# Gated expert rows go into the residual stream by accumulating stores, and the projection starts from raw rows

## What is computed

```python
def trunk(x):
    for layer in (0, 1):
        xn = rms_norm(x, mix_norm_g[layer])            # x * rsqrt(mean(x*x) + eps) * g
        x = x + (even_mixer if layer == 0 else odd_mixer)(xn)
        x = x + hierarchical_moe(rms_norm(x, ffn_norm_g[layer]))
    return x

def hierarchical_moe(xn):                              # 1024 tokens
    grp_p, grp = top_1(softmax(xn @ wg_group + b))     # 4 groups
    top_p, local = top_2(softmax(e_logits[grp]))       # 8 experts in a group
    gate = grp_p * top_p / sum(top_p)                  # two gates a token
    expert = grp * 8 + local                           # 32 experts, 2048 slots
    y[slot] = (silu(x[tok] @ w_gate[e]) * (x[tok] @ w_up[e])) @ w_down[e]
    return sum over the token's two slots of gate * y[slot]
```

## Time and profile before

| | us |
|---|---|
| median of 3 runs | 2018.22 |
| the profiled execution | 2011.2 |
| its span, first to last instruction | 2009.6 |
| PE busy in the span | 1814.2 |
| DVE busy | 1194.1 |
| ACT busy | 883.8 |
| POOL busy | 321.3 |
| mean granted clock of TensorE | 0.948 of full speed |
| DMA, mean over the span | 186 GB/s |

### The profile page before, as it was taken

One profiled execution on the slowest core, in us unless ns is written; L12 is line 12 of the kernel. 1 busy time (PEld: TensorE's weight loads), 2 busy tenths in 40 slices (PEclk: granted clock), 3 DMA queues, 4 the chain that ended last, 5 costly groups with the idle time before them and its releaser, 6 DMA issues. The chain is left out here.

```text
span 2009.6 us, 26040 instructions
## 1 busy us (share of the span) xinstructions
PE 1814.2 (90%) x9786; PEld 1498.5 (75%) x9787; DVE 1194.1 (59%) x1603; ACT 883.8 (44%) x1062; POOL 321.3 (16%) x260
## 2 busy tenths in 40 slices
PE   8999999577999999889999956999999979999990
PEld 6888889476778878768887745888878857888770
DVE  4323434566665445669999857323235558999984
ACT  4102222263333332348888844111112137888870
POOL 0000000001000001134334300000000133344320
PEclk8999999778999999989999987999999989999995
DMA  5433332702000043479999957111306369999976
GB/s 204 142 121 121 113 131 70 170 1 85 1 1 1 1 158 135 171 291 362 376 373 378 355 217 249 42 52 42 94 13 216 105 253 349 381 385 374 371 283 260
DMA packets 144946, 374.18 MB, mean 186 GB/s; under 512 B 39886, under 2 KB 74830, under 8 KB 120094
## 3 DMA queue, kind: packets, MB, share of 16 engines
q1 hardware_dynamic: 113254, 309.38, 42.3%
q0 software_dynamic: 22368, 45.47, 6.3%
q10 hardware_dynamic: 9216, 17.93, 2.4%
HBM read 331.15 MB, written 75.10 MB: 202 GB/s over the span
## 5 line engine op out<-in xcount | busy, mean ns | idle before, releaser
L1345 PE MATMUL ex_ps_h<-even_split 128*128 128x512 f32 x768 | 194.5, 404 | 7.8 <-DVE even_split L1474 7.4
L1345 PE MATMUL ex_ps_h<-odd_split 128*128 128x512 f32 x768 | 193.1, 401 | 9.0 <-DVE odd_split L1474 7.2
L1345 PEld LDWEIGHTS ex_ps_h<-even_split 128*128 128x128 f32 x768 | 141.0, 190 | 46.8 <-DVE even_split L1474 13.6
L1345 PEld LDWEIGHTS ex_ps_h<-odd_split 128*128 128x128 f32 x768 | 140.4, 189 | 47.5 <-DVE odd_split L1474 13.9
L520 PE MATMUL in_ps<-in_w_hi,in_xT_hi 128*128 128x512 f32 (+1 forms) x448 | 172.2, 384 | 1.7 <-DVE in_xT_lo L425 1.7
L520 PE MATMUL in_ps<-in_w_lo,in_xT_hi 128*128 128x512 f32 (+1 forms) x448 | 169.0, 377 | 0.0
L520 PE MATMUL in_ps<-in_w_hi,in_xT_lo 128*128 128x512 f32 (+1 forms) x448 | 169.0, 377 | 0.0
L1749 PE MATMUL conv_ps<-conv_xT_hi,conv_w_hi 128*128 128x512 f32 x384 | 150.4, 392 | 0.9 <-DVE conv_w_lo L1687 0.9
L1749 PE MATMUL conv_ps<-conv_xT_lo,conv_w_hi 128*128 128x512 f32 x384 | 149.7, 390 | 0.0
L1749 PE MATMUL conv_ps<-conv_xT_hi,conv_w_lo 128*128 128x512 f32 x384 | 149.7, 390 | 0.0
L2470 ACT ACTIVATE att_prob<-att_ps_s 128x512 f32<-128x512 f32 x114 | 68.0, 598 | 151.4 <-PE att_ps_s L2405 151.2
(11 more groups left out here) (360 smaller groups left out, 4023.7 us busy)
## 6 DMA issues: line engine op xcount, KB each, us to landing
all_region<-in_moe_w_gate SPq DMA_DIRECT2D x16, 1024.0 KB
all_region<-in_moe_w_up SPq DMA_DIRECT2D x16, 1024.0 KB
all_region<-in_moe_w_down SPq DMA_DIRECT2D x16, 1024.0 KB
experts_w_gu<-in_moe_w_gate SPq DMA_DIRECT2D x16, 1024.0 KB
experts_w_gu<-in_moe_w_up SPq DMA_DIRECT2D x16, 1024.0 KB
experts_w_d<-in_moe_w_down SPq DMA_DIRECT2D x16, 1024.0 KB, 15.4
all_region<-in_ev_w_in SPq DMA_DIRECT2D x12, 1024.0 KB, 8.3
proj<-in_stage ACTq DMA_DIRECT2D x48, 256.0 KB, 2.1
```

Source lines behind the costliest of these rows:

```text
L1345: last = pe.matmul(ps_h[:, u % 2, :], a[:, u % 2, k, :], w[:, k, :], start=(k == 0 and j == 0), stop=(k == KT - 1 and j == 2))
```

## The change

What it does, part by part:

1. **Stores that accumulate.** The experts' results are no longer written to `slots`. ACT multiplies the rows by their gates on the way out of PSUM (a scale for each partition), and POOL's indirect DMA adds them into the residual stream in DRAM (`compute_op=ALU.add`), into `stream` for layer 0 and into `out` for layer 1. The destination index is the token. Experts are taken in the order 0, 8, 16, 24, 1, 9, ... (`EXPERT_AT`), so that four stores in a row go to four groups; before each store POOL waits for the store of four experts earlier.
2. **Gates by expert.** After the softmax the router multiplies the one-hot choices by the gates (DVE), PE makes 16 more products of 128x32 that list the gates by place and expert, and DVE copies the list. PE's last warm-up goes from 8 products to 2 and 2, ahead of and behind these. `coded` (two DVE operations for each tile) replaces the code factor in `placed_at`.
3. **No mixing.** `mix` and `finish` are gone, and so are the loads of `slots` and the store of `stream1`. The convolution stage's rows are loaded by SP's queue at the end of the experts' block, after all 32 stores have landed (`MixedRows.load`); its gains and first weights are loaded there too, before that wait.
4. **Raw rows in the input stage.** PE turns the raw rows; the gain goes into the weights (ACT's high part takes it as a scale, DVE's low part as a factor, in pieces of 512 columns), and 1/rms is applied when DVE takes the product. The first product is done in two halves of four pieces. The constants are made inside this block, at the head of POOL's stream.
5. **Retention steps** come in every tile of blocks 3 to 5, none in block 6. With its places free, SP's queue loads keys, gains, `peT`, `w1s`, `w2s` and `q_rows` during block 6, before the preparation block, and preparation starts its turning and `add_places` one step earlier.

The core of the diff:

```diff
 # input stage
-                    act.activation(w_hi[:, b % 2, at, 0:n], raw[:, c, :, 0:n], ACT.Copy).then_inc(hi_ready[c], 1)
+                    for k in range(HALF):
+                        act.activation(w_hi[:, b % 2, c * HALF + k, 0:n], raw[:, c, k, 0:n], ACT.Copy,
+                                       scale=gains_T[:, c * HALF + k:c * HALF + k + 1]).then_inc(hi_ready[c], 1)
-                    dve.scalar_tensor_tensor(xn[:, t % 2, :], xin[:, t % XS, :], rstd[:, t:t + 1], gains[:],
-                                             ALU.mult, ALU.mult).then_inc(normed, 1)
-                    dve.tensor_copy(stage[:, q % 4, 0:n], ps[:, q % BANKS, 0:n]).then_inc(staged, 1)
+                    dve.tensor_scalar(stage[:, q % 4, 0:n], ps[:, q % BANKS, 0:n], rstd[:, t:t + 1], None, ALU.mult
+                                      ).then_inc(staged, 1)
-            return divmod((b - GATE) * NT + t, 4) if b >= GATE else (None, None)
+            return divmod((b - GATE) * NT + t, 3) if GATE <= b < GATE + 3 else (None, None)
+                sp.wait_ge(y_done, NT)
+                sp.wait_ge(y_ready, NT)
+                for t in range(NT - 4, NT):
+                    in_memory(sp, KEYS, t)
+                ahead.load_first_keys(sp)
+                early.load_small(sp)
+                sp.wait_ge(multiplied, (KEYS + 1) * NT)
+                early.load_weights(sp)
+                for t in range(NT):
+                    in_memory(sp, KEYS + 1, t)
+                    ahead.load_second_keys(sp, t)
 # router
+                dve.tensor_tensor(chosen[:].rearrange("p c t e -> p (c t) e"), chosen[:].rearrange("p c t e -> p (c t) e"),
+                                  gates[:].unsqueeze(2).to_broadcast([P, 2 * NT, NE]), ALU.mult).then_inc(gates_placed, 1)
-                warm_up(pe, ps_o[:, 0, 0:COLS], cst.ident[:], hT[:, (NT - 2) % 2, 0:COLS // P, :].rearrange("p k n -> p (k n)"), 8)
+                warm_up(pe, ps_o[:, 0, 0:COLS], cst.ident[:], hT[:, 0:COLS // P, :].rearrange("p k n -> p (k n)"), 2)
+                pe.wait_ge(gates_placed, 1)
+                pe.wait_ge(logits_out, NT)
+                for t in range(NT):
+                    for c in range(2):
+                        last = pe.matmul(ps_g, placed_at[:, c, t, :], chosen[:, c, t, :], start=(t == 0 and c == 0), stop=(t == NT - 1 and c == 1))
+                last.then_inc(gates_listed, 1)
+                warm_up(pe, ps_o[:, 0, 0:COLS], cst.ident[:], hT[:, 0:COLS // P, :].rearrange("p k n -> p (k n)"), 2)
 # experts
+EXPERT_AT = [s % NG * EPG + s // NG for s in range(NE)]
+                def add_rows(w, at):
+                    if at >= NG:
+                        pool.wait_ge(scattered[(at - NG) % U], w * (16 * STEPS) + (16 * ((at - NG) // U) + 16))
+                    pool.wait_ge(y_out, w * NE + (at + 1))
                     pool.sem_inc(apart, 1)
                     pool.indirect_dma_start(
-                        out=slots, out_offset=bass.IndirectOffsetOnAxis(ap=idx[:, e, 1:2], axis=0),
-                        in_=y[:, e % 2, :], in_offset=None,
-                        bounds_check=last_slot, oob_is_err=False).then_inc(scattered[e % U], 16)
+                        out=stream, out_offset=bass.IndirectOffsetOnAxis(ap=idx[:, EXPERT_AT[at], 0:1], axis=0),
+                        in_=y[:, at % 2, :], in_offset=None,
+                        bounds_check=last_token, oob_is_err=False, compute_op=ALU.add).then_inc(scattered[at % U], 16)
-                    act.activation(y[:, u % 2, :], ps_y[:], ACT.Copy).then_inc(y_out, 1)
+                    act.activation(y[:, u % 2, :], ps_y[:], ACT.Copy, scale=lists.gate[:, ds(place_of(n, u), 1)]).then_inc(y_out, 1)
-                for piece in (SECOND, DOWN):
-                    sp.wait_ge(piece_lo[piece], NE - B + 1)
-                following.load(sp, range(NT - 2))
+                if following is not None:
+                    for piece in (SECOND, DOWN):
+                        sp.wait_ge(piece_lo[piece], NE - 1)
+                    following.load_weights(sp)
+                    for u in range(U):
+                        sp.wait_ge(scattered[u], 16 * STEPS)
+                    following.load(sp)
 # convolution stage
-                    act.wait_ge(mixed, t + 1)
+                    act.wait_ge(x_loaded[t], 16)
-                    for c in range(2):
-                        last = dve.scalar_tensor_tensor(xin[:, t, :], ya[:, t % YA, c, :], gates[:, t + c * NT:t + c * NT + 1],
-                                                        xin[:, t, :], ALU.mult, ALU.add)
 # the whole
-            finish(nc, "end", following[1], slots, gates, out)
```

More of the change, by code:

```diff
@@ L507, in turn, with first_product @@
                     for k in range(KT):
-                        last = pe.transpose(ps_t[t % 2][:, k, :], xn[:, t % 2, k * P:(k + 1) * P], cst.ident[:])
+                        last = pe.transpose(ps_t[t % 2][:, k, :], xin[:, t % XS, k * P:(k + 1) * P], cst.ident[:])
                     last.then_inc(turned, 1)
+                def first_product(c):
+                    pe.wait_ge(x_high, 1)
+                    for j, (a, w_part) in enumerate(((xT_hi, w_hi), (xT_lo, w_hi), (xT_hi, w_lo))):
+                        if j == 1:
+                            pe.wait_ge(x_low, 1)
+                        for k in range(c * HALF, (c + 1) * HALF):
+                            if j != 1:
+                                pe.wait_ge((hi_ready if j == 0 else lo_ready)[c], k - c * HALF + 1)
+                            last = pe.matmul(ps[:, 0, 0:COLS], a[:, k, 0:P], w_part[:, 0, k, 0:COLS],
+                                             start=(k == 0 and j == 0), stop=(k == KT - 1 and j == 2))
+                    if c == 1:
+                        last.then_inc(multiplied, 1)
                 def product(b, t):
@@ L592 @@
 EXPERT_BUFFERS = 4
+EXPERT_AT = [s % NG * EPG + s // NG for s in range(NE)]
+PLACE_OF = [EXPERT_AT.index(e) for e in range(NE)]
 class ExpertData:
@@ L1139, in load, with landed @@
             sp.dma_start(self.rows[:, t, :], self.src[t * P:(t + 1) * P, :]).then_inc(self.loaded[t], 16)
-    def load_again(self, sp, loaded):
+    def landed(self, sp):
         for t in range(NT):
-            sp.dma_start(self.rows[:, t, :], self.src[t * P:(t + 1) * P, :]).then_inc(loaded, 16)
-def experts(nc, name, data, lists, slots, most, ident, following):
+            sp.wait_ge(self.loaded[t], 16)
+        for sem in (*self.raw_loaded, self.gain_loaded):
+            sp.wait_ge(sem, 16)
@@ L1159, in experts, with load_again @@
+    def load_again(self, sp, again):
+        self.load_first(sp, [again] * 3, again)
+        for t in range(NT):
+            sp.dma_start(self.rows[:, t, :], self.src[t * P:(t + 1) * P, :]).then_inc(again, 16)
+        sp.wait_ge(again, 16 * (NT + 4))
+def experts(nc, name, data, lists, stream, most, ident, following=None):
     U, B = 8, EXPERT_BUFFERS
@@ L1322, in landed @@
                 def landed():
-                    for t in range(NT - 2, NT):
-                        pool.wait_ge(following.loaded[t], 16)
-                later_waves(pool, full, wave, landed)
+                    if following is not None:
+                        following.landed(pool)
+                    lists.store_gates(pool)
+                later_waves(pool, full, wave, landed, lambda: pool.sem_inc(all_scattered, 1))
             @block.tensor
@@ L1536, in mix_and_conv, with constants @@
[L1536 to L1541 removed]
+def constants(pool, cst, ident_ready):
+    pool.memset(cst.ident[:], 0.0)
+    pool.memset(cst.ones[:], 1.0)
+    pool.drain()
+    pool.affine_select(out=cst.ident[:], in_=cst.ident[:], compare_op=ALU.not_equal, fill=1.0, base=0,
+                       pattern=[[-1, P]], channel_multiplier=1).then_inc(ident_ready, 1)
+    pool.affine_select(out=cst.before[:], in_=cst.ones[:], compare_op=ALU.is_gt, fill=0.0, base=0,
+                       pattern=[[1, P]], channel_multiplier=-1)
+    pool.iota(cst.iota_i[:, 0, :], pattern=[[1, 64]], base=0, channel_multiplier=0)
+    pool.iota(cst.iota_i[:, 1, :], pattern=[[1, 64]], base=-64, channel_multiplier=0)
+    pool.drain()
+    pool.tensor_copy(cst.iota[:], cst.iota_i[:, 0, :])
+    pool.tensor_copy(cst.from_64[:], cst.iota_i[:, 1, :])
+    pool.drain()
@@ L1647, in _ @@
                 act.wait_ge(eps_ready, 1)
+                act.activation(root[:, 0:1], eps[:], ACT.Sqrt)
+                high(0, 0)
                 squares(0)
@@ L1812, in prepare_attention @@
+def prepare_attention(nc, name, proj, cst, con, keep, ahead, early):
     NK = 2 * G
@@ L2640, in trunk @@
             region = Region(top)
-            with nc.Block() as block:
-                constants(nc, cst, block)
             def expert_data(layer, m, region):
@@ L2646, in expert_data @@
                                   a["moe_w_down"][layer, :, :, :], region)
-            following = [NextRows(top, f"rows{layer}_loaded", stream[2 * layer], region) for layer in range(2)]
```

(2 more changed lines are left out.)

540 lines of the change are left out of this document (266 added, 274 removed).

## The result

The changed kernel takes 2034.3 us (median of 4 runs, 2033.51 to 2035.38) against 2017.3 us of the kernel before in the same session (4 runs). The ratio is 1.0075, 95% interval 1.0052 to 1.0098: **slower, by 17 us** by the medians, where 1996 was forecast and the range ended at 2028. Its profiled execution spans 2031.8 us; the one of before spanned 2009.6.

The account below looks back on a forecast made before the run. An expert stage was taken to sit on both limits, PE and DMA, at once. Edges of -54.8 us and accumulating stores of +32.4 us gave -22.4 us, from 2018.2 to 1995.8 us; the range was 1962 to 2028 us.

Parts of the forecast that it names:

- Accumulating stores: Expert stages: each adding store costs 0.6 us of DMA time over 27 rounds while weights are outstanding, +32.4 us for two layers.
- Rival 2: Expert stages: the store is dear, DMA engines lose over 1.0 us a store; at 1.4 us 2039 us; chance 0.17.
- the edges: Places outside the expert rounds where PE stands still, from input stage to finish: together -54.8 us.
- Rival 3: Expert stages: store landing passes 17 us and ACT's wait for `y` sets the round; 2039 us at 20 us; chance 0.03.
- Rival 1: Expert stages: the destination fetch is hidden, price 0 to 0.3 us a store; 1963.4 to 1980 us; chance 0.24.
- Rival 4: Convolution's start stays put and weights hold the input stage, so -54.8 becomes -43; 2008 us; chance 0.11.
- Rounds near 10.5, waits from about round 9: Expert stages, expected sign: ACT's waits for weights begin earlier, about round 9, with rounds near 10.5 us from there on.
- Input stage: Start of the kernel: x lands sooner, and square, root and norm leave the path to the first product; -6.7 us.
- Preparation: Preparation's start: with gains, keys and table already in SBUF, DVE sums right after the squares; -9.4 us.
- Router: End of the router stage, twice: wait for gates, 16 more products and warm-ups; +1.6 us each, taken as +4 in all.
- Convolution: Convolution's start: block opens about 5 us later, but turnings come sooner without `mix`; -8 us.
- Finish: End of the kernel: without `finish` the span ends at about 1974.9 us; -34.7 us.

Follow-up runs that it names:

- the lower half: No model kernel, stores by themselves with rows on partitions 0 to 63: six beside 24 weight loads add 7.2 us plain, 14.5 us with the addition.
- even partitions: No model kernel, stores by themselves with 64 rows on every second partition: six adding stores beside 24 weight loads cost 7.0 us, 1.2 each.
- the even layout: The changed kernel with an expert's listed rows on every second partition, one line of index pattern altered: 1964.72 us, 0.9721 of before.
- a control: The changed kernel with place s on partition 127 - s, so that rows stand on partitions 64 to 127: 2045.02 us in one run.
- a spread: The changed kernel with partition p holding place (p mod 8) x 16 + p div 8: 2024.51 us, 1.0029 of before.

## Why the prediction was wrong, step by step

- **Accumulating stores, "I take 0.6", +32.4 us: this step failed.** It measured 60.5 us. The upper bound of 1.4 us a store held (1.2 beside loads); so did the mechanism that the store's DMA time lands on the path once weights are late, though not in all 27 rounds: up to the ninth copy of `y` they kept 9.3 to 10.0 us, and the 30 us a layer were lost behind it. What failed is the unit. I divided the queue's share by all 16 engines, "0.69 us of all engines", and took the 5% of mean idle time as room for the fetch. The rows of a list half in use lie on 8 engines. These had far less idle time than the mean says, and a store costs them twice the mean (2.4 us for 64 adding rows on 8 engines, 1.2 on 16). Put right, the same argument would have given 0.69 x 2 = 1.4 us, near the 1.2 us measured, and 1.4 x 54 = 76 us: slower.
- **The Trainium skill's rule in the prediction** (Collectives: The Full Stack, "The bandwidth ceiling: the fold count and why AG ≠ RS ≠ AR"), a reducing transfer pays for a second source, gave +37 us by the mean. Six adding stores on the lower half cost 14.5 us where plain ones cost 7.2: there the doubling is right, the average over engines was not. On even partitions the factor is 1.5 (7.0 and 4.8 us), with all rows 1.7 (14.6 and 8.5). That a second read is the reason no count here shows.
- **Rival 2, the dear store at 0.17, is what happened**, by its sign (over 11 us a round, ACT waiting for weights) and its time (2039 for 1.4 us; 2034.3 measured). That the time came so near is in part luck: it took 75.6 us for the addition and -54.8 for the edges, where the runs show 60.5 and -45. Its reason, unused rows that cost double, was not the one: the even layout has as many unused rows and costs half. Rival 3 did not happen: stores landed in 11.2 us and ACT never waited for one in `rows_out`. Rival 1 is true only in the even layout, where the addition's price is small. Rival 4's -43 for the edges is near the -45 of the profiles, but not for the reasons named: the convolution's start came 9.7 us nearer and the input stage lost its gain at its end.
- **Rounds near 10.5, waits from about round 9**: the waits came as foretold, at 968.52, behind the ninth copy of `y`. The rounds are 11.2.
- **Input stage, -6.7: this step failed too, -0.2.** The third turning began at 22.36 instead of 27.30, 4.9 us earlier, but the next block opens at 364.77 against 364.97. "SP's queue has nothing else" was true and not enough: the 23 issues that now load the preparation's data share the engines with the last stores, which land in 5.7 us (median of eight) instead of 1.8. The last product ends about 3.7 us earlier and the block opens 8.7 instead of 5.2 us behind it.
- **Preparation, -9.4: right** at its start (369.42 against 378.81, of which 0.2 is the block's earlier opening). Attention then begins 463.01 against 470.63, 7.6 earlier: 1.8 us are given back within the stage, and 1.0 more within attention, which the change left alone; neither was followed up.
- **Router, +4 in all: near, +4.8.** From the last score product of attention (702.81 against 709.47) to the first `y` 1.4 us are lost, and 3.4 from the convolution's last product (1518.51 against 1499.58) to the first `y` of layer 1.
- **Convolution, -8: right, -9.7.** Last store to first turning 18.5 us against 21.8, to the fifth turning 36.1 against 45.8; foretold were 18.8 and 37.2. Here "less 1 for the landing" was not needed.
- **Finish, -34.7: right, -33.4.** The last store stands 10.5 us before the end, not 9.
- **Unforeseen:** 3.5 us a layer of longer rounds where no DMA is waited for.
- **The base.** The profiled execution of before was 6 us quicker than its median, that of after near it. By the medians, 17.0 - 67.1 = -50 us for the edges, against -54.8 forecast; by the profiles -45. By the profiles the whole miss adds up: 28.1 us on the addition (60.5 for 32.4), 6.6 on the longer rounds and 9.9 on the edges, 44.6, from -22.4 forecast to +22.2 measured.
- **The range** took 1.2 us as the price's end with the edges in full, 2028. With the upper bound of 1.4 that the text itself gives, it would have been 2039 and would have held.

## What to carry to other kernels

A busy share over 16 DMA engines is a mean, and a load waits for the slowest of them: before room is read from it, ask which engines an operation uses, here by the partitions that its rows stand on. An indirect DMA of 128 rows of which about half are used, as here, should have the used ones on every second partition (or filled by bits 2, 3, 4, 6 first); that line was worth 70 us in one kernel and 11 in the other (7.1 of them from first to last `y`), and it turned a loss into the best version of this study, 1964.7 us. And where a control and a spread come from the same guess about the hardware, a run that measures the guess by itself comes first.

## What the runs showed that I had not expected

- An adding store of 128 rows of 4 KB lands in the time of one with 64 rows on the lower half, 6.1 and 6.2 us, and costs the same beside loads, 76.8 and 76.7 us a phase of 24 loads.
- On the lower half an addition doubles what a store costs: 2.4 against 1.2 us (14.5 and 7.2 us for six), and a quiet landing of 3.2 becomes 6.2. On even partitions it is 1.2 against 0.8, and 4.8 against 2.7. The profile counts the same packets and bytes for both.
- POOL is busier with it too: 2.75 us for most adding stores in the rounds of 11.2 us, about 1.8 in the even layout, 1.56 alone, where a plain one takes 1.00 alone.
- DMA's share can fall while it becomes the bound: 0.95 with TensorE as the limit, 0.94 with DMA; 1.01 in the fastest version.
